# First rows of a routed MoE fetched by token number, and another order of expert passes

## The chip, the cores and the metric

One core of one Trainium2 chip (trn2). The metric is the device time of one execution in microseconds (us); lower is better. The engines are TensorE (PE), VectorE (DVE), ScalarE (ACT), GpSimd (POOL) and SyncE (SP); SP only issues DMAs and waits. ACT and POOL issue DMAs too.

## The reference

A two-layer encoder in float32 over 528 positions (16 meta tokens and 512 frames) of width 1024:

```python
h = x + retention(rms_norm(x), w_in, w_out)      # layer 0
h = h + hier_moe(rms_norm(h), ...)
k, v = shared_kv(h)                              # then layer 1
h = h + swa_sink_attention(rms_norm(h), ..., k, v)
h = h + hier_moe(rms_norm(h), ...)
out = rms_norm(h)

# hier_moe: 4 groups of 4 experts; top-1 group, top-2 experts inside it
expert_idx = g_sel * 4 + top_2(softmax(e_logits[g_sel]))
weights    = g_w * top_p / sum(top_p)
y[token]   = sum over its 2 experts e of weight * (silu(t @ w_gate[e]) * (t @ w_up[e])) @ w_down[e]
```

An expert has 2 MB of gate and up weights and 1 MB of down weights; 16 experts in each of two layers are 100 MB.

## The kernel before

**Retention (to about 500 us)** runs on PE without a gap worth naming. Its last products, `W1_01`, `W1_23` and `W1_4` (token tiles 0 and 1, tiles 2 and 3, the meta tile), come in this order; DVE adds each to `h`, ACT squares (`squares`), POOL makes the deviation (`deviations`), DVE normalizes (`norm_tile`) into `xn`.

**Routing** (`experts` on every engine, once a layer, 5 token tiles in layer 0 and 4 in layer 1). PE transposes each tile (`transposed`), DVE scales it (`feature_major`), PE makes the logits. DVE takes the maxima in a chain of some 30 small steps, each waiting for the one before, up to the masks (`mask_ready`, L1752). PE counts the tokens of each expert before each token (bank 2, `RK`, L1040 and L1042). From the counts DVE works out the slot of each token's two choices: experts get blocks of 64 rows ("pairs") and of 32 rows ("singles"). It writes `slot_i` (L1846), builds `one_hot` (L1851, L1854), then the tables `e_of` of experts by block (L1877).

**Rows by slot.** POOL scatters each token's row of `xn` twice into DRAM `slot_rows` by `slot_i` (L2179, 10 indirect DMAs in layer 0, 8 in layer 1). Pass 0 doesn't wait for that: PE multiplies `one_hot` by `xn` (L1057, 10 or 8 float32 products of 512 columns, two records each in the trace), which leaves the first 128 slots' rows in PSUM banks 0 and 1 (`X0`), and ACT copies them to `xg`. The rows of all other passes are read from `slot_rows` by ACT's queue (`load_rows`) after all scatters.

**Passes** (`ROUNDS` = 12, each 128 rows). PAIRS_IN_PASS = (2, 1, 2, 1, 1, 2, 2, 1, 0, 2, 2, 0): a pass holds n pairs and 4 - 2n singles. PE, for k from 1: `gate_up(k)` (64 records, L1080), `hidden_to_features(k - 1)` (L1087), `rows_to_features(k + 1)` (L1068), `down_project(k - 1)` (L1099). DVE scales the transposed rows (`widen`, L1547).

**Weights** lie in six slots, expert number j in slot j mod 6. Five are filled with a guess (`GUESSED`: all but slot 3) while routing runs. Slot 3 has its 2 MB where `xn` lies, and SP loads it after all scatters. SP loads number j + 6 into the slot of number j when the pass with single j is through: gate and up after that pass's `gate_up`, down after its `down_project`. In SP's program the loads stand in the order of the passes. Before the guessed weights are used, a conditional DMA loads another expert where the guess was wrong; POOL issues such conditional DMAs for the singles (`singles_weights`), and a pass with singles waits for those of the pass in which the same numbers were pairs (`weights_arrived`). SP also loads the first half of the attention's `w_q` after pass 9 of layer 0.

**After the passes** POOL gathers both choices' rows of each token from `slot_out` (L2211) and DVE adds them.

Of the kernel before, what the change touches and what calls it, by code (L numbers as in the profile page):

```python
# [19 lines left out]
D = 1024  # L20
KT = D // 128
# [16 lines left out]
ROWS_SLOT = 3  # L38
GUESSED = [4, 5, 0, 1, 2]
# [6 lines left out]
PAIRS_IN_PASS = (2, 1, 2, 1, 1, 2, 2, 1, 0, 2, 2, 0)  # L46
# [48 lines left out]

def most_blocks(tokens):

    return max((2 * tokens + (BLK - 1) * m) // BLK for m in range(2, EXPERTS + 1))
# [3 lines left out]
assert PASSES[0] == [("pair", 0), ("pair", 1)] and PASSES[-1] == [("single", EXPERTS - 4 + n) for n in range(4)]  # L102
# [10 lines left out]
NCONST = C_DECAY + HEADS * N_META  # L113
# [6 lines left out]
def tables():  # L120
# [15 lines left out]
    c[:, C_EPS] = EPS  # L136
    r = np.zeros((128, NRT), f)
# [103 lines left out]
def build(nc, a, out):  # L241
# [4 lines left out]
    with ctx:  # L246
# [23 lines left out]
        slot_g = sb("slot_g", [128, 2, 5], I)  # L270
        ps = ctx.enter_context(nc.psum_tensor("ps", [128, 8, 512], F))
# [89 lines left out]
        logit_f = arena[:, cv.at:cv.at + POS]  # L361
# [11 lines left out]
        one_hot = xg[:, 1, 0:640].rearrange("p (t s) -> p t s", t=5)  # L373
        xgT = x_words[:, 2 * D:4 * D].rearrange("p (n k c) -> p n k c", n=2, k=KT)
        cv.at = 5 * D + KT * POS
        gat_at = {0: 14336, 1: 16384, 2: 27392, 3: 10240}
        gat = [(x_words[:, 0:2 * D] if t == META else arena[:, gat_at[t]:gat_at[t] + 2 * D]).rearrange("p (n c) -> p n c", n=2)
# [27 lines left out]
        slot_out = nc.dram_tensor("slot_out", (LATE, D), F).ap()  # L405

# [16 lines left out]
        MOE_TILES = [[0, 1, 2, 3, META], [0, 1, 2, 3]]  # L423
# [21 lines left out]
        def moe_plan(l):  # L445
            fl.phase([(f"m{l}_{t}", 2 * (n % 2)) for n, t in enumerate(MOE_TILES[l])])
            fl.phase([(f"LT{l}_{t}", 4 + n % 2) for n, t in enumerate(MOE_TILES[l])])
            fl.phase([(f"LG{l}", 6), (f"RK{l}", 2), (f"X0_{l}", 0)])
# [44 lines left out]
        def sigs(names, tag):  # L493
# [5 lines left out]
        mo = [sigs("eg_in eg_out d_in d_out mask_ready eb_ready slot_ready scattered "  # L499
                   "tanh_done y_out0 y_out1 x_in0 x_in1 "  # L500
                   "gathered0 gathered1 gathered2 gathered3 gathered4 gath_used gather_ready late_ready", f"_{l}") for l in range(2)]
        gu_in, down_in = ([sem(f"{n}{s}") for s in range(W_SLOTS)] for n in ("gate_up_in", "down_in"))
# [12 lines left out]
        def gu(k):  # L515

            return {0: ring[:, 0], 1: gu_arena[:, 0], 2: gu_arena[:, 1], 3: gu_rows, 4: ring[:, 1], 5: ring[:, 2]}[k % W_SLOTS]
# [55 lines left out]
        def out_chunk_used(eng, n):  # L573

            if n % 2:
                fl.wait_full(eng, f"W{n // 2}_4")
            else:
                eng.wait_ge(wo_used, n // 2 + 1)
# [19 lines left out]
        G44 = POSN  # L598
# [7 lines left out]
        B_ROWS, B_HID, B_YA, B_YB = 0, 5, 6, 7  # L606

# [15 lines left out]
        def rows_loaded(k):  # L623

            return groups_until(k, 1)
# [64 lines left out]
        def _(sp):  # L690
# [41 lines left out]
            def first_weights(l, ready):  # L732
# [4 lines left out]
                rest = [j for j in (0, 1, 2, 4, 5) if j not in ready]  # L737
# [6 lines left out]
                for j in (2, 4, 5):  # L744
                    down_weights(l, j, j)

            def experts(l, beside=lambda k: None):
# [5 lines left out]
                for j in sorted(GUESSED):  # L753
# [7 lines left out]
                fl.wait_full(sp, f"X0_{l}")  # L761
# [23 lines left out]
            first_weights(0, {4: chunk_used(2), 5: lambda: None, 0: chunk_used(3)})  # L785

            def attention_loads(k):
# [3 lines left out]
                if k == last_use(5) + 1:  # L791
                    sp.dma_start(ring[:, W_Q[0]], a["w_q"][0]).then_inc(q_in[0], 16)
# [14 lines left out]
            first_weights(1, {5: lambda: fl.wait_full(sp, f"Qa{NT - 1}"), 0: lambda: fl.wait_full(sp, f"Qb{NT - 1}"),  # L807
# [12 lines left out]
        def _(pe):  # L820
# [158 lines left out]
            for hf in range(2):  # L979
                groups = [(f"W{hf}_01", (0, 1)), (f"W{hf}_23", (2, 3)), (f"W{hf}_4", (META,))]  # L980
                for c in range(2):
                    n = 2 * hf + c
                    pe.wait_ge(y_split, HEADS if hf or c else HEADS - 1)
# [26 lines left out]
            def experts(l):  # L1010
# [25 lines left out]

                n = EXPERTS * (5 - l)
# [21 lines left out]
                last.then_inc(full[0], 1)  # L1059
# [3 lines left out]
                def rows_to_features(k):  # L1063
                    if k:
                        pe.wait_ge(m[f"x_in{k % 2}"], rows_loaded(k))
# [46 lines left out]
                rows_to_features(1)  # L1112
                for k in range(1, ROUNDS):
# [161 lines left out]
        def _(act):  # L1275
# [114 lines left out]
            def experts(l, ready):  # L1390
                m = mo[l]
                squares(MOE_TILES[l], nrm[f"_m{l}"], moe_junk[l], ready)
                for t in MOE_TILES[l]:
# [4 lines left out]
                act.wait_ge(m["eg_in"], 1)  # L1398
                nc.scalar.activation(view(EG, 5 - l, 4), view(EG, 5 - l, 4), ACT.Exp).then_inc(m["eg_out"], 1)
                act.wait_ge(m["d_in"], 1)  # L1400
                nc.scalar.activation(view(DX, 5 - l), view(DX, 5 - l), ACT.Exp).then_inc(m["d_out"], 1)
# [42 lines left out]
                fl.wait_full(act, f"X0_{l}")  # L1444
                nc.scalar.activation(xg[:, 0, :], flat(ps[:, 0:2, :]), ACT.Copy).then_inc(free[0], 1)
                act.wait_ge(m["scattered"], 16 * 2 * (5 - l))
                load_rows(1)
# [843 lines left out]
```

## Time and profile before

| | |
|---|---|
| median of 3 runs | 1155.47 us (1153.18 to 1155.6) |
| the profiled execution, its own time | 1156.74 us |
| its span | 1155.1 us |
| PE busy | 1061.4 us, 92% of the span |
| moved by DMA | 200.87 MB |
| DMA queues q1 (SP, POOL's direct ones), q10 (ACT), q0 (POOL's indirect ones) | 151.26, 31.63, 17.04 MB |

A busy PE is not PE at its peak: the records overlap. Times in the traces are microseconds from the start of the span. "Idle before" of a record names what ended the engine's wait. The chain of waits is followed back from the last instruction.

### The profile page before, as it was taken

The numbers are of one execution on the slowest core, as the hardware profiler recorded it, in microseconds if no ns is written. First come the engines' busy times: TensorE is split into PE (matmuls) and PEld (weight loads), VectorE is DVE, ScalarE is ACT, GpSimd is POOL, SyncE is SP. The second block draws the span as 40 slices with busy tenths as digits, with TensorE's granted clock in tenths as the row PEclk, the third lists the DMA queues.
The fourth block names the chain that finished last, engine by engine and source line by source line (L and its number), as shares of the span: only waits on it lengthen the run. The fifth ranks groups of instructions, "written<-read, shape, count | busy, mean of one in ns | idle before, by whom it ended". The sixth has DMA issues, their size and how long they took to land.

```text
span 1155.1 us, 16343 instructions
## 1 busy us (share of the span) xinstructions
PE 1061.4 (92%) x6528; PEld 669.8 (58%) x6528; DVE 465.7 (40%) x831; ACT 248.4 (22%) x479; POOL 238.7 (21%) x232
## 2 busy tenths in 40 slices
PE   4999999999999999987899997989998987999992
PEld 3989979979988877763333332445444453333331
DVE  6400424234236651046223225657547736132217
ACT  5122133114214321020011111314214410011111
POOL 5323314305314524003000005510000002000005
PEclk8999999999999999998899998999999998999996
DMA  7232223114114121366799896130003057899946
GB/s 296 74 128 74 74 80 121 54 45 155 56 37 164 37 73 73 146 264 278 249 358 395 339 397 232 73 146 1 1 1 146 1 233 312 319 366 354 374 198 230
DMA packets 34836, 200.87 MB, mean 174 GB/s; under 512 B 4352, under 2 KB 4480, under 8 KB 25808
## 3 DMA queue, kind: packets, MB, share of 16 engines
q1 hardware_dynamic: 21168, 151.26, 33.9%
q10 hardware_dynamic: 8864, 31.63, 7.7%
q0 software_dynamic: 4736, 17.04, 4.0%
q8 instruction: 47, 0.77, 0.3%
q14 instruction: 21, 0.17, 0.0%
HBM read 303.59 MB, written 28.44 MB: 287 GB/s over the span
## 4 chain that ended last, share of the span: by engine, by line
PE 78%; DVE 13%; ACT 3%; issue 3%; DMA 2%; POOL 1%; POOLq 0%; ACTq 0%; DVEq 0%
PE ps L843 29%; PE ps L1080 15%; PE ps L1099 7%; PE ps L968 4%; PE ps L1204 4%; PE ps L1146 3%; PE ps L849 2%; DVE arena L2075 2%; PE ps L1068 2%; DVE arena L2072 2%; PE ps L1057 2%; PE ps L1018 1%; PE ps L912 1%; ACT arena L1507 1%; PE ps L1164 1%
## 5 line engine op out<-in xcount | busy, mean ns | idle before, releaser
L843 PE MATMUL ps<-x_hi,ring_r 128*128 128x264 f32 x1024 | 190.9, 287 | 2.5 <-DVE xT L1547 2.5
L2155 POOL TENSOR_TENSOR ring_r<-ring,ring_r 128x1024 fp32r<-128x1024 f32 x56 | 134.8, 2422 | 272.3 <-ACT ring_r L1296 272.3
L843 PEld LDWEIGHTS ps<-x_hi,ring_r 128*128 128x128 f32 x1024 | 160.2, 189 | 3.1 <-issue 2.9
L1080 PE MATMUL ps<-arena,xT 128*32 128x512 f32 x864 | 157.8, 600 | 0.0
L1080 PE MATMUL ps<-ring,xT 128*32 128x512 f32 x672 | 143.7, 602 | 5.9 <-DVE xT L1547 5.9
L843 PE MATMUL ps<-xT_r,ring_r 128*128 128x264 f32 x512 | 146.1, 285 | 0.0
L1547 DVE TENSOR_TENSOR xT<-ps,gains 128x512 f32<-128x512 f32 (+1 forms) x76 | 47.1, 661 | 188.4 <-PE ps L1068 178.5
L843 PE MATMUL ps<-ring_r,x_hi 128*128 128x512 f32 x320 | 100.7, 396 | 0.0
L843 PEld LDWEIGHTS ps<-xT_r,ring_r 128*128 128x128 f32 x512 | 96.9, 189 | 0.1
L1099 PE MATMUL ps<-arena 128*32 128x512 f32 x624 | 87.3, 595 | 4.3 <-ACT arena L1421 4.3
L1296 ACT ACTIVATE ring_r<-ring 128x1024 fp32r<-128x1024 f32 x56 | 57.9, 1054 | 118.1 <-PE ps L843 70.8
L1080 PEld LDWEIGHTS ps<-arena,xT 128*32 128x32 f32 x864 | 41.6, 111 | 54.9 <-issue 54.4
L1080 PEld LDWEIGHTS ps<-ring,xT 128*32 128x32 f32 x672 | 37.9, 111 | 60.7 <-issue 60.2
L843 PEld LDWEIGHTS ps<-ring_r,x_hi 128*128 128x128 f32 x320 | 60.1, 188 | 13.8
L2143 POOL TENSOR_SCALAR var<-ss 128x1 f32<-128x1 f32 (+1 forms) x23 | 8.8, 384 | 237.9 <-ACT arena L1284 230.3
L1164 PE MATMUL ps<-ring,xT 128*128 128x512 f32 x128 | 56.1, 595 | 0.0
L968 PE MATMUL ps<-arena 128*128 128x264 f32 (+4 forms) x256 | 47.8, 334 | 0.0
L1099 PEld LDWEIGHTS ps<-arena 128*32 128x32 f32 x624 | 22.6, 109 | 43.1 <-issue 41.4
L1284 ACT ACTIVATE arena<-h 128x1024 f32<-128x1024 f32 (+1 forms) x23 | 24.3, 1057 | 103.3 <-DVE h L1936 48.0
L1421 ACT ACTIVATE arena<-ps 128x256 f32<-128x256 f32 x24 | 9.2, 384 | 167.5 <-PE ps L1087 162.9
L968 PEld LDWEIGHTS ps<-arena 128*128 128x128 f32 (+1 forms) x256 | 41.1, 189 | 6.8
L1507 ACT ACTIVATE arena<-arena 128x256 f32<-128x256 f32 x64 | 31.6, 494 | 62.6 <-DVE arena L2080 62.6
(266 smaller groups left out, 1567.9 us busy)
## 6 DMA issues: line engine op xcount, KB each, us to landing
arena<-in_w_gu SPq DMA_DIRECT2D x22, 2048.0 KB, 14.7
ring<-in_w_gu SPq DMA_DIRECT2D x20, 2048.0 KB
arena<-in_w_down SPq DMA_DIRECT2D x36, 1024.0 KB
arena<-in_w_gu POOLq DMA_DIRECT2D x18, 2048.0 KB
ring<-in_w_gu POOLq DMA_DIRECT2D x14, 2048.0 KB
arena<-in_w_down POOLq DMA_DIRECT2D x26, 1024.0 KB
ring<-in_w_ret SPq DMA_DIRECT2D x48, 512.0 KB, 3.6
ring<-in_w_ret_out SPq DMA_DIRECT2D x16, 512.0 KB, 4.4
```

Of the source, the lines that this page charges most:

```text
L843: last = mm(dst, a_parts[x], b_parts[y], start=(start and n == 0), stop=(stop and n == 2))
L968: last = mm(ps[:, b + g, c - lo:HALF], v_tm[0:r, t, 128 * m:128 * m + 128], scores_of(t)[0:r, c - 128 * t:hi - 128 * t], start=(t == 0), s ...
L1080: last = mm(ps[cols, b, :], xgT[:, k % 2, c, cols], by_row(gu(j))[:, c, :], start=(c == 0), stop=(c == KT - 1))
L1099: last = mm(ps[cols, b, :], hidT[:, c, cols], down(j)[:, c, 512 * n:512 * n + 512], start=(c == 0), stop=(c == 1))
L1146: last = mm(ps[0:rows(t), b, :], xTk[:, k, col0(t):col0(t) + rows(t)], w_kv[:, k, :], start=(k == 0), stop=(k == KT - 1))
L1164: last = mm(ps[:, b, :], xT[:, k, col0(t):col0(t) + 128], w_q[c][:, k, :], start=(k == 0), stop=(k == KT - 1))
L1204: last = mm(ps[:, b + c, :], oT1[:, k, :], w[:, k, :], start=(k == 0), stop=(k == KT - 1))
L1284: nc.scalar.activation(junk[0:r], h[0:r, t, :], ACT.Square, accum_out=ss[0:r, t:t + 1]).then_inc(sig["sq_done"], 1)
L1296: nc.scalar.activation(w_hi[to][:, m], w_raw[slot][:, m], ACT.Copy).then_inc(hi_made, 1)
L1507: nc.scalar.activation(P[:, hd, :], P[:, hd, :], ACT.Exp, bias=nmx[:, hd:hd + 1], accum_out=sm[:, hd:hd + 1]).then_inc(p_exp, 1)
L1547: return V_.tensor_tensor(dst[:, 4 * g:4 * g + 4, c0:c0 + r], src, gains[:, gain, 4 * g:4 * g + 4].unsqueeze(2).to_broadcast([128, 4, r]), ...
L2155: G.tensor_tensor(w_lo[slot][:, m], w_raw[slot][:, m], w_hi[to][:, m], ALU.subtract).then_inc(lo_made, 1)
```

## The change

Pass 0 gets no rows from PE any more. The normalized rows are also stored as they are, by token, in DRAM `token_rows` (ACT's queue, 5 and 4 stores of up to 512 KB). For passes 0, 1 and 2, `one_hot[k]` (slots of pass k) is multiplied by one column of token numbers; ACT casts the 128 sums to `token_i`, and POOL gathers 128 rows by them from `token_rows` into `xg`. DVE works out the slots that lie in pairs first (`first_place`), builds `one_hot[0]`, then the two rows of `e_of` that SP needs, then `one_hot[1]`, and only then the other slots, `slot_i` and `one_hot[2]`.

The order of passes starts 2, 2, 0, 2, 1 pairs, so that each of the first three passes is one run of slots. Slot 5 instead of slot 3 has its weights in the place of `xn`. In layer 0 the meta tile comes third: `W1_4` ahead of `W1_23`. ACT instead of DVE scales the features of pass 0. PE multiplies constants in four places.

```diff
-PAIRS_IN_PASS = (2, 1, 2, 1, 1, 2, 2, 1, 0, 2, 2, 0)
+PAIRS_IN_PASS = (2, 2, 0, 2, 1, 2, 2, 1, 0, 2, 2, 0)
-ROWS_SLOT = 3
-GUESSED = [4, 5, 0, 1, 2]
+ROWS_SLOT = 5
+GUESSED = [0, 1, 2, 3, 4]
+GATHERED = 3
-        MOE_TILES = [[0, 1, 2, 3, META], [0, 1, 2, 3]]
+        MOE_TILES = [[0, 1, META, 2, 3], [0, 1, 2, 3]]
 # SP: the rest of slot 5, and w_q
                 sp.wait_ge(mo[l]["scattered"], 16 * 2 * (5 - l))
-                fl.wait_full(sp, f"X0_{l}")
                 gate_up_weights(l, ROWS_SLOT, e, cond=wanted)
-                if k == last_use(5) + 1:
+                if k == last_use(3):
                     sp.dma_start(ring[:, W_Q[0]], a["w_q"][0]).then_inc(q_in[0], 16)
 # PE
+                constant_products(5)
                 pe.wait_ge(m["mask_ready"], 1)
...
-                for _ in range(9):
-                    mm(ps[:, 4, :], ident, con[:, 0:512], start=True, stop=True)
-                pe.wait_ge(m["slot_ready"], 2)
-                for c in range(2):
-                    for i, t in enumerate(tiles):
-                        last = mm(ps[:, c, :], one_hot[0:rows(t), t, :], xn[0:rows(t), t, 512 * c:512 * c + 512],
+                def tokens_of(k):
+                    pe.wait_ge(hot_ready, GATHERED * l + k + 1)
+                    for i, t in enumerate(tiles):
+                        last = mm(ps[:, B_TOKENS[k], 0:1], one_hot[k][0:rows(t), t, :], con[0:rows(t), C_TOKEN + t:C_TOKEN + t + 1],
                                   start=(i == 0), stop=(i == len(tiles) - 1))
+                    last.then_inc(tokens_made, 1)
+                constant_products(5)
+                tokens_of(0)
+                constant_products(3)
+                tokens_of(1)
+                constant_products(1)
...
                 rows_to_features(0)
                 gate_up(0)
                 rows_to_features(1)
+                tokens_of(2)
 # ACT
+                def store_rows(n):
+                    t = MOE_TILES[l][n]
+                    act.wait_ge(nrm[f"_m{l}"]["xn_done"], n + 1)
+                    act.dma_start(token_rows[128 * t:128 * t + rows(t), :], xn[0:rows(t), t, :]).then_inc(rows_stored, 16)
...
+                def first_features():
+                    round_full(act, l, B_ROWS, 0)
+                    for c in range(KT):
+                        last = nc.scalar.activation(xgT[:, 0, c, :], ps[:, c // 4, 128 * (c % 4):128 * (c % 4) + 128], ACT.Copy,
+                                                    scale=gains[:, G_MOE[l], c:c + 1])
+                tokens_of(0)
+                tokens_of(1)
+                first_features()
                 tanh_of(0)
-                load_rows(2)
+                tokens_of(2)
                 for k in range(1, ROUNDS):
-                    load_rows(k + 2)
+                    if k > 1:
+                        load_rows(k + 2)
                     hidden_of(k - 1)
                     tanh_of(k)
                     results_of(k - 1)
+                    if k == 1:
+                        act.wait_ge(m["scattered"], 16 * 2 * (5 - l))
+                        load_rows(k + 2)
 # DVE, in routing, after D_, ID and P1
+                step(V_.scalar_tensor_tensor(v(PC, nt, 16), per_expert(P0), float(PAIR), pos, ALU.mult, ALU.add))
+                step(V_.tensor_scalar(v(G64, 16), v(D_, 16), float(PAIR), None, ALU.mult))
+                step(V_.tensor_tensor(v(DBL, nt, 16), pos, per_expert(v(G64, 16)), ALU.is_ge))
+                step(V_.scalar_tensor_tensor(v(PC, nt, 16), v(DBL, nt, 16), float(ENC_D), v(PC, nt, 16), ALU.mult, ALU.add))
... (two products with the choices' masks, two sums over experts: first_place)
+                slots_of_pass(0, first_place)
... (rows 0 and 2 of e_of)
+                slots_of_pass(1, shifted)
... (the rest of the slots as before, slot_i)
+                slots_of_pass(2, shifted)
 # POOL
+                def gather_rows(k):
+                    pool.wait_ge(tokens_read, GATHERED * l + k + 1)
+                    if k == 0:
+                        pool.wait_ge(rows_stored, 16 * (5 * l + len(tiles)))
+                    if k == 2:
+                        round_full(pool, l, B_ROWS, 0)
+                    G.indirect_dma_start(xg[:, k % 2, :], None, token_rows,
+                                         bass.IndirectOffsetOnAxis(token_i[:, l, k:k + 1], 0)).then_inc(rows_gathered[k], 16)
+                gather_rows(0)
+                gather_rows(1)
                 pool.wait_ge(m["slot_ready"], 1)
-                for t in tiles:
+                for n, t in enumerate(tiles):
+                    if n == 2:
+                        gather_rows(2)
```

## Rows read from the trace of the kernel before

**Rows 1.** The page: each engine's busy time and share.

```profile
PE 1061.4 (92%) x6528; PEld 669.8 (58%) x6528; DVE 465.7 (40%) x831; ACT 248.4 (22%) x479; POOL 238.7 (21%) x232
```

**Rows 2.** Timeline, end of retention, layer 0: start, us, engine, line, count [idle before].

```profile
496.61 1.23 DVE L1687 TENSOR_TENSOR h<-ps,h 128x1024 f32<-128x1024 f32 x1 [5.46 <-PE ps L843]
...
504.93 3.18 PE L1018 MATMUL ps<-xT,wr 128*20 128x128 f32 x16 [2.92 <-DVE xT L1547]
```

**Rows 3.** Timeline, routing of layer 0, same columns.

```profile
522.99 0.74 PE L1040 MATMUL ps<-arena,con 128*128 128x96 f32 x2 [5.48 <-DVE arena L1752]
...
523.53 2.21 PE L1042 MATMUL ps<-arena,con 128*128 128x80 f32 x10
...
525.84 0.44 DVE L1775 TENSOR_TENSOR arena<-ps,con 128x272 f32<-128x272 f32 x1 [1.77 <-PE ps L1042]
...
535.38 0.17 DVE L1846 CAST slot_i<-arena 128x10 int32<-128x10 f32 x1
...
536.56 1.40 DVE L1854 SCALAR_TENSOR_TENSOR xT<-con,arena,xT 128x128 f32<-128x128 f32 x5
...
538.02 9.43 PE L1057 MATMUL ps<-arena,xT 128*128 128x512 f32 x20 [2.63 <-DVE xT L1854]
...
547.33 0.84 POOL L2179 DMA_INDIRECT slot_rows<-arena,slot_i  x1 [0.30 <-issue]
```

**Rows 4.** Chain of waits, passes of layer 0: start, us, what.

```profile
551.13 9.77 PE ps L1080 x64
...
563.39 7.07 PE ps L1080 x64
570.47 0.37 PE ps L1087 x2
570.84 0.87 PE ps L1068 x8
571.71 3.57 PE ps L1099 x32
...
623.05 7.00 PE ps L1080 x64
```

**Rows 5.** Chain of waits, layer 1, routing and passes.

```profile
957.09 0.45 DVE arena L1775
...
968.69 8.85 PE ps L1057 x16
...
981.20 7.07 PE ps L1080 x64
...
1050.42 7.00 PE ps L1080 x64
```

**Rows 6.** POOL's indirect scatters (L2179), from issue to landing.

```profile
DMA to landing us min/median/max: 3.3/4.3/4.8
```

**Rows 7.** POOL's indirect gathers (L2211), from issue to landing.

```profile
DMA to landing us min/median/max: 2.8/6.1/6.6
```

**Rows 8.** Groups of ACT by form: count | busy us, mean ns | idle before.

```profile
L1474 ACT ACTIVATE xT<-ps,gains 128x128 f32<-128x128 f32 x32 | 8.7, 381 | 7.6 <-DVE arena L1547 7.6
```

**Rows 9.** Timeline of SP's DMA issues, passes of layer 0.

```profile
570.78 0.33 SPq L679 DMA_DIRECT2D ring<-in_w_gu  x1
...
606.22 0.94 SPq L679 DMA_DIRECT2D ring<-in_w_gu  x2
...
672.41 0.46 SPq L792 DMA_DIRECT2D ring<-in_w_q  x1
```

**Rows 10.** All DMA queues from 600 to 620 us, passes of layer 0.

```profile
DMA packets 889, 8.45 MB, mean 423 GB/s; under 512 B 108, under 2 KB 108, under 8 KB 455
```

**Rows 11.** Chain of waits, after the last pass of layer 0.

```profile
694.67 6.03 DMA slot_out<-arena
```

**Rows 12.** Windows: length, busy PE, PEld, DVE, ACT, POOL, granted clock, DMA share, GB/s.

```profile
529.00:536.00 7.00, 6.39 (x15) 2.56 (x13) 6.42 (x37) 0.00 (x0) 0.14 (x1) 0.98 0.02 7
...
550.00:555.00 5.00, 3.87 (x20) 1.15 (x24) 0.98 (x2) 0.00 (x0) 0.00 (x0) 0.50 0.46 107
```

More of the change, by code:

```diff
@@ L93, in groups_until, with first_slot @@
     return 16 * sum(len(row_groups(p)) for p in range(first, k + 1) if p % 2 == k % 2)
+def first_slot(k):
+    (_, slots), = row_groups(k)
+    return slots.start
 def most_blocks(tokens):
@@ L101 @@
 assert most_blocks(POS) <= 3 * EXPERTS and ROUNDS % 2 == 0
-assert PASSES[0] == [("pair", 0), ("pair", 1)] and PASSES[-1] == [("single", EXPERTS - 4 + n) for n in range(4)]
+assert PASSES[:2] == [[("pair", 2 * k + n) for n in range(2)] for k in range(2)]
+assert PASSES[2] == [("single", n) for n in range(4)] and PASSES[-1] == [("single", EXPERTS - 4 + n) for n in range(4)]
 assert all(pass_of("pair", j) < pass_of("single", j) for j in range(EXPERTS))
@@ L575, in out_chunk_used @@
             if n % 2:
-                fl.wait_full(eng, f"W{n // 2}_4")
+                fl.wait_full(eng, "W0_4" if n == 1 else "W1_23")
             else:
@@ L736, in first_weights @@
                     gate_up_weights(l, j, j)
-                rest = [j for j in (0, 1, 2, 4, 5) if j not in ready]
+                rest = [j for j in GUESSED if j not in ready]
                 for j in rest[:2]:
@@ L1035, in experts, with constant_products @@
                 last.then_inc(full[6], 1)
+                def constant_products(n):
+                    for _ in range(n):
+                        mm(ps[:, B_YB, :], ident, con[:, 0:512], start=True, stop=True)
+                constant_products(5)
                 n = EXPERTS * (5 - l)
@@ L1695, in _ @@
                 V_.tensor_tensor(hh, ps[SHORT:SHORT + N_META, b, :], hh, ALU.add).then_inc(free[b], 1)
+            add_rows(0, "W0_01", 0)
+            add_rows(0, "W0_23", 2)
+            add_meta(0)
+            add_rows(1, "W1_01", 0)
+            for n in range(2):
+                norm_tile(nrm["_m0"], n, MOE_TILES[0][n], xn)
+            add_meta(1)
+            norm_tile(nrm["_m0"], 2, META, xn)
+            add_rows(1, "W1_23", 2)
             def experts(l):
@@ new lines, in experts, with slots_of_pass @@
+                step.wait()
+                for n in range(2):
+                    step.done(V_.tensor_reduce(first_place[:, n, 0:nt], in_pairs[:, n], X, ALU.add))
+                step.wait()
+                iota = con[:, C_IOTA:C_IOTA + 128]
+                def slots_of_pass(k, where):
+                    for t in range(nt):
+                        step.done(V_.tensor_scalar(one_hot[k][:, t, :], iota, where[:, 0, t:t + 1], None, ALU.is_equal))
+                    step.wait()
+                    for t in range(nt):
+                        last = V_.scalar_tensor_tensor(one_hot[k][:, t, :], iota, where[:, 1, t:t + 1], one_hot[k][:, t, :],
+                                                       ALU.is_equal, ALU.add)
+                    last.then_inc(hot_ready, 1)
@@ L2175, in experts @@
                     pool.wait_ge(s_zeroed, 32 * HEADS)
-                for t in tiles:
+                for n, t in enumerate(tiles):
+                    if n == 2:
+                        gather_rows(2)
                     r = rows(t)
```

154 lines of the change are left out of this document (83 added, 71 removed).

## Prediction

> **What bounds the kernel now.** I read the page first. PE is busy for 92% of the span [rows 1], so the question is where PE waits, and whether the change shortens that or adds to it. The chain of waits says where: inside retention and inside the passes it is PE alone; around routing it hops between DVE, PE and ACT. In layer 0 PE waits 5.48 us for the masks and 1.77 us of DVE time pass until the counts are in; from then DVE works 12.1 us (525.84 to 537.96) until `one_hot` is ready, PE multiplies for 9.4 us, and pass 0 starts at 551.13 [rows 3, 4]. In layer 1 the same stretch runs from 957.09 to 981.20 [rows 5]. Third, the timeline ahead of that: PE waits 2.92 us for DVE before the first logits, because DVE normalizes two more tiles and adds the meta tile first [rows 2]. Fourth, a pass: 7.07 + 0.37 + 0.87 + 3.57, near 11.9 us, all PE [rows 4]. Last the DMA side, which PE's 92% hides: in a stretch of the passes all 16 engines together move 423 GB/s, filled [rows 10], while ahead of the scatters they stand idle (share 0.02) [rows 12]. Weights are 50 MB a layer, so passes are PE's by a small margin only.
>
> **Part 1, tile order.** `W1_23` ends last, near 500.3 instead of 496.6, its add of 1.23 us ends at 501.6, and DVE scales tile 0 at once (1.3). Logits start near 502.9 instead of 504.93, and without 2.92 us of idle time the first tile's logits may run in 1.9 instead of 3.18 us. The five row stores lie beside this on ACT's queue, the last landing 20 us before anyone needs them. Between -1.5 (norms of the last two tiles now come between the scalings) and -3.3 I take -2.7. Layer 1 keeps its order: 0.
>
> **Part 2, constant products ahead of the masks.** Ten records in the 5.48 us in which PE waits. They keep PE at 2.4 GHz, so that counting (0.74 + 2.21 us, after idling) takes some 1.7. I take -1.2 and -0.9; if the clock were at 1.2 GHz there, they would end 3 us after the masks. Bounds -1.4 and +3.
>
> **Part 3, the first slots ahead of all others.** After the counts: the comparison (0.44), a sum, scan and minimum, seven steps of 0.2 to 0.4 us, and ten `one_hot` steps (2.4 us, as now: 535.5 to 537.96), about 5.8 us where there were 12.1: -6.3. In layer 1 11.6 becomes 5.2: -6.4.
>
> **Part 4, one column instead of 512.** Removed: from 538.02 to 551.13, 13.1 us (12.5 in layer 1). Added: ten records of one column, priced by the counting products, 0.22 each: 2.0 (1.6 in layer 1; below, 1.3); ACT's cast 0.25; start of POOL 0.3; the gather; transposes 1.1; eight ACT steps; 0.15. The gather is 512 KB by indirect DMA. Full scatters land in 4.3 us, gathers at the end of a layer in 6.1, but those queue behind each other [rows 6, 7]. I take 5. ACT's eight steps start every 0.27 us with 0.38 for the last: 2.2 [rows 8]. Sum 11.0 and 10.7: -2.1 and -1.9. The gather of pass 1 follows 4.6 us of DVE later and its products end 0.1 before the first rows land, so this cover is just used up.
> The Trainium skill, *DMA: Bandwidth & Descriptors*, section "Anatomy of one DMA", gives 2.0 us and the bytes at 436 GB/s, an estimate of 3.2 us for this gather where the rows have 4.3 and 6.1. By it the rows would land 1.8 us sooner and PE would still be in the second token product: nothing would be gained.
>
> **Where pass 0 starts.** Layer 0: 2.7 + 1.2 + 6.3 + 2.1 = 12.3 earlier, at 538.8. Layer 1: 9.2 earlier, at 972.0. That is the whole gain, 21.5 us. Now what it triggers.
>
> **Part 5, into pass 2.** The third token product (2.0 us) comes after the transposes of pass 1, where PE now idles 1.45 us for DVE: +0.5 and +0.15. PE would reach `gate_up(2)` at 561.1 and 994.0. `slot_i` comes later by the work put ahead of it: near 540.0 and 973.5. POOL issues an indirect DMA every 1.27 us (535.86 to 547.33, nine steps) [rows 3]: four scatters, then it waits for the third tokens (549.6; 982.3), then that gather and six (four) more scatters. The last scatters land near 561.5 and 991.6. Behind them on POOL stand the conditional DMAs: singles 0 to 3 are now in pass 2 and wait for those of pass 1, which wait for those of pass 0. Bounds for such an empty DMA are 0 and, from the shortest direct landing, some 2 us; with 2 I get 563.5 in layer 0, so +2.4, and 0 in layer 1. The gather of pass 2 lands near 554 and 988, before its turn. ACT stands in its queue at the scatters before it loads pass 3's rows; with slot 5's 3 MB in flight they land some 2 to 3 us late, but PE has a longer wait ahead, which takes this up.
>
> **Part 6, the weights' queue.** This is where I expect the gain to go. Now numbers 6 and 7 are loaded from 570.78, the end of pass 1's `gate_up`, 8 and 9 two passes later, 10 from 606.22 [rows 9], and the down weights of 8 and 9 come behind number 10. With four singles in pass 2, SP issues gate and up of 6, 7, 8, 9 after `gate_up(2)`, their down weights after `down_project(2)`, and number 10, needed in pass 6, behind all eight. That is 4 x 2.1 + 4 x 1.05 + 2.1 = 14.7 MB, and rows in and out of 3.5 passes at 1.05 MB, 3.6: 18.3 MB. At 423 GB/s 43.3 us [rows 10]; with issue and flow 2.5 and the receipt, 46. PE needs only 40.9 from the end of `gate_up(2)` to pass 6. So from 570.4 the weights are there at 616.4, and slot 5, loaded only after the scatters and ahead in the queue, makes it 617.5 (in layer 1 1047.5). Before, pass 6 starts at 623.05 and 1050.42 [rows 4, 5]. Of 12.3 and 9.2 there remain 5.5 and 2.9: -8.4.
> The rule that speaks against the change is in the same page of the Trainium skill, "Issuing engines are not separate DMA queues": a gather on POOL's queue or a store on ACT's adds no bandwidth. The rows agree so far as all queues together stay at 423. With its ceiling of 436 GB/s the sum would be 1.3 us less in each layer, an estimate.
>
> **Part 7, clock.** In layer 0 pass 0 takes 9.77 us where all others take 7.07, since the clock granted was 0.50 (1.2 GHz) after short waits; layer 1 had the same waits and no drop [rows 4, 5, 12]. A drop costs 2.7. There are now four such places, pass 0 and pass 6 of either layer; my count above has none, the run before has one (which is in its 623.05). I take 1.4 drops: +3.8, bounds 0 and 10.8.
>
> **Part 8, `w_q`.** From 672.41 it moves behind pass 11, just ahead of the last store of results, on the path now with 6.03 us [rows 9, 11]. 2.1 MB beside a 0.5 MB store and POOL's gathers: 0 if they take turns without loss, 4 if the gathers are shifted by most of its 5 us. I take +1.5.
>
> **Sum.** -8.4 + 3.8 + 1.5 = -3.1 on the profiled execution's own 1156.74: 1153.6. The median of the runs is 1.3 lower, so 1152.4.
>
> **The rivals.**
> *The passes keep pace.* If number 10 is there in time (a full queue does better than 423, or less has to move), pass 6 starts at 611.3 and 1041.8 and -20.3 stays; with half the clock cost and `w_q`, about -16: 1139.5. Against it: it takes 18.3 MB in 38 us, 480 GB/s, and no row shows that.
> *PE's clock eats the rest.* If both waits before pass 0 and both before pass 6 end at 1.2 GHz, +10.8 in place of 3.8, so +3.9: 1159.4. For it: the waits before pass 6 are 5 to 6 us, and after the 5.48 us wait for the masks the clock was low. It decides from three drops on.
> *The first rows come late.* The gather takes 8 us beside the tail of the guessed weights and the stores, or SP's conditional loads for slot 1 hold pass 0. Then pass 0, and all behind it, is 3 us later in each layer: +2.9: 1158.4. Against it: DMA stands idle from 529 [rows 12].
> *The late `w_q` costs its full 4:* 1155.
>
> **How the numbers follow.** Forecast 0.50, its own range 1147 to 1157; passes keep pace 0.17; clock 0.16; late rows 0.10; `w_q` 0.07. A measurement here tells about 0.2% (2.3 us) from nothing. Of the forecast 0.29 lies below that, 0.11 within, 0.10 above; with the first rival 0.46 is faster; same is 0.11 + 0.05 + 0.04 = 0.20; the rest, 0.34, is slower. For 8 in 10 the range reaches into the first rival and over the second and third: 1143 to 1162.
>
> **What would show it.** Right: pass 0 near 539 and 972; on PE a wait before pass 6 released by the load of gate and up weights, some 5 us; a DMA share of 0.9 and more from pass 2 to 6; the first logits near 503. Wrong if PE has no wait at pass 6 (then faster), if pass 2 waits over 3 us for POOL's conditional loads, if token products come out at far more than 2 us, or if pass 0 waits for weights and not for ACT.

## The result and the profile after

The changed kernel takes 1171.8 us (median of 4 runs, 1171.11 to 1172.68) against 1155.49 of the kernel before beside it: ratio 1.0139, 95% interval 1.0127 to 1.0151. It is 16 us slower. The prediction said 1152.4, 1143 to 1162.

The chain of waits of layer 0 after the change (start, length, what; all in us). It begins with the last product of retention and ends in pass 0; the first and last line are cut by the view's ends. Its first L1038 is the second tile's; the logits of the first tile start at 504.30:

```profile
496.00 5.79 PE ps L861 x25
...
501.81 1.23 DVE h L1744
...
507.22 1.92 PE ps L1038 x16
...
521.41 0.46 PE ps L1065 x2
521.88 1.06 PE ps L1067 x10
...
523.03 0.45 DVE arena L1843
...
527.48 1.41 DVE xT L1878 x5
...
528.93 1.46 PE ps L1079 x10
530.42 0.18 ACT token_i L1490
530.60 0.29 issue
530.89 5.51 DMA xT<-token_rows,token_i
...
536.54 1.08 PE ps L1099 x8
537.64 2.18 ACT xT L1495 x8
539.82 0.14 issue
539.96 5.30 PE ps L1111 x21
```

Up to here the change did what it was to do: pass 0 starts at 539.96 where it started at 551.13 [rows 4], 11.2 us earlier. The same chain through the first passes:

```profile
552.47 7.07 PE ps L1111 x64
...
560.79 3.61 PE ps L1130 x32
...
565.66 11.36 DMA xT<-slot_rows
577.01 0.04 issue
577.06 1.97 PE ps L1099 x8
579.03 4.10 PE ps L1130 x32
583.12 6.87 PE ps L1111 x64
...
607.14 7.00 PE ps L1111 x64
...
619.12 8.36 issue
627.48 8.93 PE ps L1111 x64
```

Two waits are new. PE is done with pass 2's `gate_up` and waits 5.46 us for the rows of pass 3; it then waits 8.36 us before pass 6 (L1111 at 627.48, where the kernel before had 623.05 [rows 4]). In layer 1 pass 0 starts at 980.73 (before 981.20, but this layer's routing began 7.6 us late), the wait before pass 3 is 8.61 us, and the one before pass 6 only 0.6; pass 6 starts near 1063.5 instead of 1050.42 [rows 5]:

```profile
970.52 5.78 DMA xT<-token_rows,token_i
976.44 1.96 PE ps L1099 x8
978.41 2.18 ACT xT L1495 x8
980.73 9.79 PE ps L1111 x64
...
1006.47 14.24 DMA xT<-slot_rows
1020.76 1.97 PE ps L1099 x8
1022.73 4.11 PE ps L1130 x32
```

A balance by the starts of passes: routing of layer 0 gives 11.2, its passes 0 to 11 lose 17.6 (pass 11 starts at 688.7, before 682.3), the rest of layer 0 loses 1.2, routing of layer 1 gives 8.0, its passes lose 14.5. That is 14.1 us lost by pass 11 of layer 1; the spans, 1168.9 and 1155.1, are 13.8 apart.

What the DMA engines do between the end of `gate_up(2)` and pass 6 (this view gives busy time of each engine, the granted clock, the DMA share, and GB/s):

```profile
572.00:627.50 55.50, 42.08 (x364) 14.94 (x366) 14.10 (x32) 5.39 (x15) 0.44 (x10) 0.91 1.01 387
```

All 16 engines are busy throughout and move 387 GB/s, not the 423 of [rows 10]: 21.5 MB, of which 16.9 on the weights' queue and 4.5 on ACT's. The sum of the prediction had 18.3 MB at 423. While the rows of pass 3 are on their way, from 566 to 577, the queues moved:

```profile
q1 hardware_dynamic: 272, 3.14, 73.0%
q10 hardware_dynamic: 313, 1.15, 28.3%
```

The columns are packets, MB and share. SP (q1) had issued slot 5's 3 MB at 565.29 and 565.91, ACT (q10) a store of results at 565.21 and the rows at 565.66. Both queues got about as many packets (from 568 to 576, 217 each), but q10's hold 3.7 KB on average and q1's 11.5. So ACT's queue, with 0.5 MB of store ahead of 0.5 MB of rows, moved 0.1 MB a microsecond. The Trainium skill, *DMA: Bandwidth & Descriptors*, section "Queues, rings and completion order", says that each DMA engine goes round the queues packet by packet; 313 packets beside 272 agree with it.

### The profile page after: what moved, and what is told of

Its sections match the earlier page's. It is cut to its first block, busy times and chain, and to the rows that moved or that the text cites. A ratio compares the mean times of both kernels' runs of the same rounds, so it can differ in the third digit from the quotient of the medians.

```text
span 1168.9 us, 16499 instructions
## 1 busy us (share of the span) xinstructions
PE 1061.4 (91%) x6566; PEld 672.2 (58%) x6566; DVE 475.5 (41%) x881; ACT 251.5 (22%) x499; POOL 242.6 (21%) x238
## 4 chain that ended last, share of the span: by engine, by line
PE 74%; DVE 12%; DMA 7%; issue 3%; ACT 3%; POOL 0%; ACTq 0%; POOLq 0%; DVEq 0%
PE ps L861 29%; PE ps L1111 13%; PE ps L1130 7%; PE ps L986 4%; DMA xT<-slot_rows 4%; PE ps L1236 4%; PE ps L1178 3%; PE ps L867 3%; PE ps L1099 2%; DVE arena L2163 2%; DVE arena L2160 2%; PE ps L930 1%; ACT arena L1565 1%; DVE h L2024 1%; PE ps L1196 1%
## 5 line engine op out<-in xcount | busy, mean ns | idle before, releaser
L1111 PE MATMUL ps<-ring,xT 128*32 128x512 f32 x768 | 162.7, 620 | 13.7 <-issue 8.9
L1111 PE MATMUL ps<-arena,xT 128*32 128x512 f32 x768 | 160.8, 609 | 1.0 <-DVE xT L1605 1.0
L1605 DVE TENSOR_TENSOR xT<-ps,gains 128x512 f32<-128x512 f32 (+1 forms) x72 | 44.4, 658 | 190.9 <-PE ps L1099 183.3
L1111 PEld LDWEIGHTS ps<-ring,xT 128*32 128x32 f32 x768 | 43.9, 114 | 92.4 <-issue 91.9
L1111 PEld LDWEIGHTS ps<-arena,xT 128*32 128x32 f32 x768 | 42.4, 112 | 36.0 <-issue 35.6
```

What stands on the lines that cost most here:

```text
L1111: last = mm(ps[cols, b, :], xgT[:, k % 2, c, cols], by_row(gu(j))[:, c, :], start=(c == 0), stop=(c == KT - 1))
L1605: return V_.tensor_tensor(dst[:, 4 * g:4 * g + 4, c0:c0 + r], src, gains[:, gain, 4 * g:4 * g + 4].unsqueeze(2).to_broadcast([128, 4, r]), ...
```

## The experiments

All ratios are to the kernel before, run on the same chip beside each group; intervals are at 95%. The changed kernel has 1.0139. The start of a pass is that of its `gate_up`'s first product.

**e1: all scatters ahead of the third gather.**

```diff
                 for n, t in enumerate(tiles):
-                    if n == 2:
-                        gather_rows(2)
...
+                gather_rows(2)
                 pool.wait_ge(m["eb_ready"], 2)
```

> The changed kernel, with one line moved: POOL issues the gather for pass 2 behind all scatters instead of behind the first four. Queue theory (the scatters land at 565.3 where they landed before 552, so slot 5's 3 MB and all loads behind them start late and the DMA engines stay full until pass 6): the scatters land near 557.5, slot 5 is loaded before ACT asks for the rows of pass 3, PE's wait before the transposes of pass 3 falls from 5.5 and 8.8 us to under 1 us and pass 6 starts some 6 us sooner in both layers: about 1160 us. Clock theory (the loss is low clock after waits, wherever they are): waits only move to pass 2, whose rows come 1 to 2 us later; 1170 to 1173 us. Theory that row loads are slow whatever lies beside them: the wait before pass 3 stays over 4 us, 1169 to 1172 us.

1174.3 us, 1.0164 (1.0134 to 1.0194). None of the three was right. The wait before pass 3 is gone in both layers, as the queue theory said, but PE waits 8.4 and 9.0 us before pass 6, which starts at 626.3 and 1064.7: 1.2 us sooner in one layer and 1.2 later in the other. And `gate_up(1)` starts at 556.15 instead of 552.47, at low clock: the third token product, ten products of one column, is strung out over 5.8 us while the scatters run. Nothing that the profile shows released PE in these gaps:

```profile
550.92 0.38 PE L1079 MATMUL ps<-con,arena 128*128 128x1 f32 x2 [1.25 <-issue]
552.34 0.16 PE L1079 MATMUL ps<-con,arena 16*128 16x1 f32 x1 [1.03 <-issue]
553.05 1.08 PE L1079 MATMUL ps<-con,arena 16*128 16x1 f32 x4 [0.56 <-issue]
```

**e2: slot 5's 2 MB of gate and up weights never loaded.**

```diff
+                _, never = expert_of(0)
...
-                gate_up_weights(l, ROWS_SLOT, e, cond=wanted)
+                gate_up_weights(l, ROWS_SLOT, e, cond=never)
```

> The changed kernel, but the 2 MB of gate and up weights of number 5 are never loaded (its products are made from what lies there; all else is loaded and done as before). Queue theory: 2 MB less ahead of the rows of pass 3 and of numbers 6 to 10, some 5 us of DMA at 423 GB/s in each layer: the wait before pass 3 nearly goes and pass 6 starts 5 us sooner, so 1161 to 1163 us. If the waits hang on when PE releases the slots and not on bytes: the first wait goes, and the second grows by as much, 1169 to 1172 us.

1166.12 us, 1.0093 (1.0062 to 1.0124). 5.7 us less, but of an expected 9 to 11. The wait before pass 3 falls to 1.2 and 0.9 us. Pass 6 starts at 620.3 in layer 0, 7 us sooner, yet PE still waits there: 6.5 and 7.7 us. So slot 5's bytes count, they are most of what delays the rows of pass 3, and they are not the whole cause of the wait before pass 6.

**e3: only the order of passes changed, with the old front.**

```diff
-ROWS_SLOT = 3
+ROWS_SLOT = 5
-PAIRS_IN_PASS = (2, 1, 2, 1, 1, 2, 2, 1, 0, 2, 2, 0)
+PAIRS_IN_PASS = (2, 2, 0, 2, 1, 2, 2, 1, 0, 2, 2, 0)
-                if k == last_use(5) + 1:
+                if k == last_use(3):
```

> The kernel before (rows of pass 0 as products of 512 columns, no gathers by token), with only the order of passes 2, 2, 0, 2, 1 and with it slot 5 in place of slot 3 as the one loaded after the scatters, and w_q behind pass 11. Theory that the order costs by itself (four numbers' weights asked for at once after pass 2, 12 us later than the first two before): pass 0 at 551 and 981 as before, pass 6 near 629 and 1056, so +12 us and 1.5 for w_q: 1165 to 1170 us. Theory that the order is harmless and only the early start with late scatters hurts: 1155 to 1158 us.

1180.89 us, 1.022 (1.0189 to 1.025), 24 us slower than the kernel before. The order costs by itself, and more than the range said. Its chain in layer 0 has no wait before pass 3, and this before pass 6 (the last line is cut by the view's end; the whole `gate_up` takes 8.61 us):

```profile
612.07 7.00 PE ps L1081 x64
...
624.15 8.01 issue
632.16 8.16 PE ps L1081 x57
```

Layer 1 has 7.74 us at the same place. Of the 24 us these two and their clock are some 19, and w_q 2 to 3. This is the largest finding: the change is two changes, an order that costs about 24 us from the old front, and an early front that brings pass 0 about 19 us forward in the two layers together. Of these 19 only some 9 are left at the end (1180.89 to 1171.8): the waits take the rest. The front with the old order was not run, since the order is what makes the first three passes one run of slots.

**e4: tile order and constant products in the kernel before; e14: tile order alone.**

```diff
-        MOE_TILES = [[0, 1, 2, 3, META], [0, 1, 2, 3]]
+        MOE_TILES = [[0, 1, META, 2, 3], [0, 1, 2, 3]]
+                for _ in range(5):      # e4 only
+                    mm(ps[:, 7, :], ident, con[:, 0:512], start=True, stop=True)
                 pe.wait_ge(m["mask_ready"], 1)
```

> The kernel before, with only the tile order of layer 0 (meta tile third, W1_4 ahead of W1_23) and five constant products ahead of the masks (parts 1 and 2 of the prediction). By my terms 2.7 us and 1.2 in layer 0, 0.9 in layer 1; scatters and all loads move with it, so the gain is kept: 1150.5 to 1151.5 us. Theory that the passes of the kernel before are already set by the weights' queue whatever starts earlier: at most 1 us, 1154.5 to 1155.5 us.

> The kernel before with the tile order of layer 0 alone (part 1), no constant products. My term: masks, slots and scatters 2.7 to 3.1 us sooner in layer 0, nothing in layer 1, so 1152.5 to 1153 us against 1155.5 to 1156.5. If the weights' queue or the clock takes it up: no change.

e4: 1154.27 us, 0.9983 (0.997 to 0.9996), some 2 us. e14: 1152.97 us, 0.997 (0.9958 to 0.9983), 3.2 us and near its term. The constants did not add to that. PE's timeline in e4 shows the reason (the bracket is the idle time before and what ended it):

```profile
533.79 14.02 PE L1061 MATMUL ps<-arena,xT 128*128 128x512 f32 x20 [4.46 <-DVE xT L1866]
```

and in e14:

```profile
535.75 9.63 PE L1059 MATMUL ps<-arena,xT 128*128 128x512 f32 x20 [2.27 <-DVE xT L1864]
```

With constants `one_hot` is ready 2.0 us sooner, but the constant products behind the counts also end sooner; PE stands idle for 4.46 us, and the products of pass 0's rows run at a granted clock of 0.50 (534 to 542) for 14.0 instead of 9.6 us.

**e5: number 10's gate and up weights ahead of the down weights of 8 and 9.**

```diff
                         gate_up_weights(l, j, e, cond=wanted)
+                        if j == 10:
+                            for late in (8, 9):
+                                e, wanted = chosen[late]
+                                down_weights(l, late, e, cond=wanted)
```

> The changed kernel, but SP issues the down weights of numbers 8 and 9 behind the gate and up weights of number 10, which pass 6 needs first, instead of ahead of them. Queue theory (number 10 is asked for only at the end of gate_up(4) and stands behind 4.2 MB of down weights asked for one pass earlier): 2.1 MB less ahead of it is 5 us at 423 GB/s, so the wait before pass 6 falls from 8.4 to some 3.5 us in layer 0 and as much in layer 1; the wait before pass 3 stays: 1160 to 1163 us. Theory that all queued bytes share the engines, so that order in SP's queue does not matter: 1170 to 1173 us.

1162.07 us, 1.0052 (1.0033 to 1.007), 9.7 us less than the change from one move in SP's queue. SP's DMAs, and PE's chain past pass 6, where no wait stands any more:

```profile
597.93 1.23 SPq L702 DMA_DIRECT2D arena<-in_w_down  x2
605.16 0.33 SPq L698 DMA_DIRECT2D ring<-in_w_gu  x1
605.77 0.94 SPq L702 DMA_DIRECT2D arena<-in_w_down  x2
606.99 0.33 SPq L698 DMA_DIRECT2D arena<-in_w_gu  x1
```

```profile
609.91 7.00 PE ps L1115 x64
...
618.16 3.57 PE ps L1134 x32
621.73 0.16 PE ps L1143
621.89 7.00 PE ps L1115 x64
```

Order in the queue matters. The wait before pass 3 stayed in sum (8.6 and 5.2 us, for 5.5 and 8.6); that it is what gives number 10 its time is argued here, and e13 bears on it.

**e6: the order 2, 2, 0 four times.**

```diff
-PAIRS_IN_PASS = (2, 2, 0, 2, 1, 2, 2, 1, 0, 2, 2, 0)
+PAIRS_IN_PASS = (2, 2, 0, 2, 2, 0, 2, 2, 0, 2, 2, 0)
```

> The changed kernel with the pass order 2, 2, 0 four times over, so that pass 6 needs numbers 8 and 9 and no longer 9 and 10; numbers 10 to 13 are asked for after pass 5 and needed from pass 7. Order theory (the wait before pass 6 comes from number 10 alone): no wait before pass 6, the waits before pass 3 stay at 5.5 and 8.8 us; 10 and 11 land some 5 us ahead of pass 7: 1153 to 1157 us. Theory that the DMA engines are behind by some 8 us whatever the order: the wait moves to pass 7, 1168 to 1173 us.

1154.14 us, 1.0003 (0.9978 to 1.0027): the whole loss is gone by this line. The ten runs lie in two groups, six from 1151.6 to 1155.5 and four from 1160.3 to 1161.9; the trace is of the first, and what parts them is open. The waits before pass 3 stay (5.4 and 3.7 us). Pass 6 starts at 618.1 and 1045.2, pass 7 at 630.1 and 1057.3, 12 us apart, so no wait moved to pass 7.

**e7: the third token product inside `gate_up(0)`.**

```diff
                     for c in range(KT):
+                        if k == 0 and c == 5:
+                            tokens_of(2)
```

> The changed kernel, but PE makes the third token product inside gate_up(0), after five of its eight steps, and ACT casts it before the tanh of pass 0, so that POOL's third gather and the scatters behind it start some 5 to 6 us sooner. Theory that the scatters' lateness (they stand on POOL behind the third gather) makes slot 5's loads and PE's wait before pass 3: scatters land near 559.5, wait before pass 3 under 1 us, pass 6 follows the end of gate_up(2) by 49 us instead of 55: 1157 to 1160 us. Theory that more DMA work beside pass 1 slows PE there (as with all scatters first): pass 1 starts 3 to 5 us later and eats it: 1168 to 1173 us.

1165.12 us, 1.0074 (1.0051 to 1.0096). 6.7 us of an expected 12 to 15. The third gather is issued at 547.26 instead of 552.66, pass 6 starts at 619.5, 48.8 us behind the end of `gate_up(2)`, as said. But the rows of pass 3 still take 9.35 us to land and PE waits 3.4 us: ACT issues them behind the results of pass 0, at 565, however early the scatters are. In layer 1 PE's wait before pass 3 falls from 8.6 to 1.5 us, and the one before pass 6 grows from 0.6 to 7.9.

**e8: e7, the order of e6, and w_q behind the last gathers.**

```diff
-                if k == last_use(3):
-                    sp.dma_start(ring[:, W_Q[0]], a["w_q"][0]).then_inc(q_in[0], 16)
...
             sp.wait_ge(mo[0]["gathered3"], 32)
+            sp.dma_start(ring[:, W_Q[0]], a["w_q"][0]).then_inc(q_in[0], 16)
```

> Three edits together: the third token product inside gate_up(0), the pass order 2, 2, 0 four times over, and the first half of w_q loaded behind the last gathers of layer 0 instead of beside the last store of results. If the three causes are the ones named and independent: no wait before pass 3 (7 us a layer with its clock), none before pass 6 (10 and 9 us), and 3 us less at the end of layer 0: 1135 to 1141 us, ahead of both kernels. If the DMA engines are the bound of passes 3 to 7 in any order, a wait of 5 us or more stands somewhere before pass 7 in each layer: 1148 to 1156 us.

1144.04 us, 0.9897 (0.988 to 0.9913), faster than both kernels. Passes start at 539.9, 552.2, 563.9, 577.6 and then every 12.0 us. It missed its range because pass 0 still runs at low clock in both layers, pass 3 waits 1.8 us, and pass 10 of layer 1 waits 2.0 us.

**e9: SP loads the rows of pass 3 ahead of slot 5's weights.**

```diff
                 sp.wait_ge(mo[l]["scattered"], 16 * 2 * (5 - l))
+                round_full(sp, l, B_ROWS, 1)
+                for place, src in row_groups(3):
+                    sp.dma_start(xg[place, 1, :], slot_rows[src, :]).then_inc(mo[l]["x_in1"], 16)
                 gate_up_weights(l, ROWS_SLOT, e, cond=wanted)
```

> The changed kernel, but SP itself loads the rows of pass 3 as soon as the scatters have landed, ahead of slot 5's 3 MB; ACT no longer does. Theory that these rows are slow because they share the engines with slot 5's load: they land within 4 us of 565.3, PE's wait before pass 3 falls from 5.5 and 8.8 us to 2 us at most (then for slot 5's weights), and passes 3 to 5 start 4 to 6 us sooner. Queue theory for the rest: number 10's weights land no sooner, so the wait before pass 6 grows by what the first lost, and the total moves by 0 to -3 us: 1168 to 1171.5 us. Theory that the two waits add up independently: 1158 to 1161 us.

1176.65 us, 1.0182 (1.0161 to 1.0203). The rows, issued at 562.61, land in 3.3 us instead of 11.4, PE waits for nothing before pass 3, passes 3 to 5 of layer 0 start 7.5 us sooner, and all but 2.3 us of it is waited out before pass 6:

```profile
599.76 7.00 PE ps L1114 x64
...
611.58 0.16 PE ps L1142
611.74 13.46 issue
625.20 9.70 PE ps L1114 x64
```

Layer 1 has 12.82 us there. The length of the wait does not set what the clock costs behind it: `gate_up(6)` takes 9.70 us after 13.46, 8.38 after 12.82, and in e12 9.97 after 4.51, for 8.93 after 8.36 in the changed kernel. The median is 5 us worse than the change's, though the profiled span is only 1.7 us longer (1170.6 against 1168.9); the expectation (0 to -3) had neither.

**e10: e8 with constant products in PE's idle places; e11: e10 with e9's edit; e12: e11 with the change's own order and e5's edit.**

```diff
-                constant_products(5)
+                constant_products(6)
                 tokens_of(0)
...
-                constant_products(1)
+                constant_products(1 + l)
...
                 rows_to_features(0)
+                constant_products(2)
                 gate_up(0)
```

> Third tokens early, periodic order and w_q last (the run before that took 1144.0), and constant products in PE's idle places ahead of pass 0: one more before the first token product, one more before the transposes of pass 0 in layer 1, two while ACT scales the features. Clock theory: pass 0 is granted 2.4 GHz and takes 7.1 us instead of 9.8 and 9.9, nothing behind it takes this back, -5.4 us: 1138 to 1140 us. Theory that the clock was lost earlier, in the wait for the masks or for the gather, and these don't bring it back: 1143 to 1146 us.

> As the run with constants, and SP loads the rows of pass 3 ahead of slot 5's weights. The last wait of the first layer's passes (1.8 us, before pass 3) goes: 1.5 to 2.5 us below the run with constants, 1136 to 1138 us. If slot 5's weights, now later, hold pass 3 instead: no change against it.

> The change's own pass order 2, 2, 0, 2, 1, with the down weights of 8 and 9 behind number 10, third tokens early, constants, w_q last, SP loading the rows of pass 3 first. If the order of passes is not itself at fault, but number 10's place in SP's queue and the late rows: as fast as with the periodic order, 1136 to 1141 us. If the order leaves too little time for number 10: a wait of 3 us or more before pass 6 in each layer, 1143 us or more.

e10: 1143.31 us, 0.9888 (0.9872 to 0.9905); e11: 1145.24 us, 0.9892 (0.9868 to 0.9916); e12: 1148.93 us, 0.993 (0.9911 to 0.9949). In e10 the clock came back, as PE's timeline shows (a pair of products in 0.62 us, not 1.07):

```profile
537.47 1.88 PE L1058 MATMUL ps<-con 128*128 128x512 f32 x4
540.00 0.62 PE L1112 MATMUL ps<-ring,xT 128*32 128x512 f32 x2 [0.64 <-ACT xT L1496]
```

Pass 1 then starts 11.1 and 10.7 us behind pass 0 instead of 12.3 and 12.4. Yet the medians of e8 and e10 differ by only 0.7 us, and the intervals of their ratios overlap. In layer 0 nothing is left of it at pass 3 (578.0, in e8 577.6): `gate_up(1)` in layer 0 takes 8.9 us instead of 7.1, at full clock and with scatters beside it, and pass 3 in layer 1 waits 2.45 us for its rows. e11 took pass 3's wait away and was not faster. e12 shows the order's own share when all else is mended: pass 6 waits 4.5 and 4.4 us, and it is 5.6 us behind e10.

**e13: e5 and e9 together.** Both diffs above.

> The changed kernel with two edits together: the down weights of 8 and 9 behind number 10's gate and up weights, and SP loading the rows of pass 3 ahead of slot 5's. The first alone took 1162.1, the second alone was no gain. Queue theory: without the 5.5 and 8.8 us of waiting before pass 3, PE reaches pass 6 at some 616 and number 10's weights, now 2.1 MB nearer, land near 619 to 620: 2 to 4 us better than the first edit alone in each layer, 1154 to 1158 us. If the waits only trade places in every form: 1160 to 1164 us. If they are independent: 12 us and more, under 1151 us.

1164.27 us, 1.0068 (1.0044 to 1.0093), so no better than e5 (1.0052). The waits only trade places: in layer 0 `gate_up(3)` waits 3.6 us for slot 5's weights, pass 6 waits 6.1 us, and starts at 620.7 where e5 had 621.9; in layer 1 pass 6 waits 7.5 us.

**e15: w_q behind the last gathers, alone.** Diff as in e8.

> The changed kernel with the first half of w_q loaded behind the last gathers of layer 0 instead of beside the last store of results (part 8). The store lands 6.2 us after its issue instead of 8.9, the gathers follow, nothing waits for w_q: 2.5 to 3.5 us, 1168.5 to 1169.5 us. If the layer's end is set by the gathers' own time: 1171 to 1173 us.

1168.04 us, 1.0103 (1.0084 to 1.0123): 3.8 us less by the medians. The last store, in e15 and in the changed kernel:

```profile
698.48 5.92 DMA slot_out<-arena
```

```profile
701.12 8.87 DMA slot_out<-arena
```

## Why the prediction was wrong

**The front (parts 1 to 4): right in sum, pass 0 at 539.96 for 538.8, and in layer 1 8.0 us gained for 9.2.** Part 1: the first logits start at 504.30, for 502.9, and the first tile's take 1.92 us, for 1.9. The 1.4 us between lie ahead of the part: in this trace retention's last product ends near 501.8, for 500.3. The count starts 1.6 us earlier than before, for 2.7. PE comes to the transposes behind retention 1.5 us later here than before, 0.9 in e14 and 0.1 in e4, and there the counts start 2.2 and 3.0 us earlier: from the end of retention on, the tile order gives 3.1 us in all three. Why retention ends at different times is not shown. Part 2: counting takes 1.5 for 2.8 us, 1.3 gained for 1.2; that PE's idle time can cost its clock where long products follow is seen in e4. Part 3: from the counts to `one_hot` 5.9 us, for 5.8. Part 4: 11.03 us from `one_hot` to pass 0, for 11.0, with token products of 1.46 (for 2.0) and a gather of 5.51 and 5.78 (for 5). In layer 1 it is 11.75, for 10.7: the transposes ran at low clock (1.96 us, for 1.1). The cover named for it was not quite there: with the row stores beside them the guessed weights keep the DMA engines busy until some 534.5, not 529. The gathers took 0.5 and 0.8 us more than the term, so the rival of late first rows (3 us a layer) is not what happened; that the weights caused these 0.5 and 0.8 is argued.

**Part 5 is the first step that failed, by its size**, in the sentence that the rows of pass 3 "land some 2 to 3 us late, but PE has a longer wait ahead, which takes this up". The scatters land at 565.3 for 561.5, as the third gather ahead of them is issued at 552.66 for 549.6 (pass 0 at low clock). The rows then share the engines with 3 MB in larger packets and take 11.4 and 14.2 us, for about 7; PE waits 5.5 and 8.6 us, and the transposes and the down products behind the wait run at low clock. e9 shows it: issued ahead of slot 5's load and of ACT's store of results they land in 3.3 us. e2 parts the two: with the store still ahead and 2 of slot 5's 3 MB gone, 1.2 and 0.9 us of wait are left. That the wait ahead takes this up was right in kind: e9 takes the wait before pass 3 away and the kernel is no faster. What the lateness cost is in the next part, since slot 5's load stands ahead of number 10. The term for POOL's conditional loads (+2.4) did not occur.

**Part 6 named the mechanism and sized it too small.** It said that number 10 stands behind eight other loads and that pass 6 waits; it waits. But pass 6 starts at 627.5, for 617.5, and in layer 1 at 1063.5, which is 1055.9 without the 7.6 us by which that layer began late, for 1047.5. So the two come 10.0 and 8.4 us later than forecast, of which the front has 1.2 and 1.1; the profiled execution's own time was 17.5 us above the 1153.6 forecast for it. In layer 0 the 10.0 are 0.8 by which `gate_up(2)` ends late (571.2 for 570.4), 3.0 for the queue without slot 5 (49 us as in e1, e3 and e7 below, for 46), and 6.2 for slot 5's load (7.3 for 1.1). In layer 1 PE lost the time at pass 3 and hardly waits at pass 6; with the first wait gone or small (e1, e7, e9) it stands before pass 6 there too, 9.0, 7.9 and 12.8 us.

Two sizes were off. The rate: 387 GB/s and not 423 over the stretch, which makes 47.3 us of 18.3 MB instead of 43.3. And the bytes: 21.5 MB, since part of slot 5's 3 MB was still queued at 572 and ACT's queue moved 4.5 MB, for 3.6. (That 21.5 / 387 gives the 55.5 us of the stretch proves nothing, as the rate was had by dividing the two.) What shows it is the runs in which slot 5's load is asked for 11 us or more before the end of `gate_up(2)` (e1, e3, e7): 19.0 to 19.5 MB then move at 388 to 400 GB/s, and pass 6 follows by 49.2, 48.9 and 48.8 us, against the 46 of the prediction and the 40.9 that PE needs. In e12, with 2.1 MB of down weights behind number 10, it is 45.3.

The rate came from too short a stretch. The 20 us of [rows 10] had stores and rows in them as well, 1.4 of 8.5 MB (17%, and 21% in the changed kernel), so 423 was not the rate of weights alone. But from 571 to 623 us the kernel before had (same columns as above):

```profile
571.00:623.00 52.00, 52.00 (x469) 18.01 (x468) 15.51 (x34) 6.71 (x17) 0.53 (x12) 1.00 0.95 374
```

That is 374 GB/s at a DMA share of 0.95, an estimate of some 394 for a full one. The DMA engines of the kernel before were busy for 95% of this stretch, so there was little room for more to be asked for at once.

The two failures are not a sum but one budget. e1, e9 and e13 take the first wait away and get it back at pass 6; e5 takes the second away while the first remains. What comes nearest to ending both is to ask for less before pass 6 (e6) and to start the scatters sooner (e7): e8 does both, and of the waits before passes 3 and 6 only 1.8 us in layer 0 is left. With the change's own order and everything else mended, 4.5 and 4.4 us before pass 6 remain (e12). e3 against the kernel before shows that the order costs some 24 us from the old front, e6 against the change that another order with the same front gives back 1.4%, some 16 us.

**Part 7:** lost clock, counted by what passes took above 7.07 and 3.57: 2.7 in pass 0 of layer 1 (in layer 0 the kernel before had it too), 0.5 in the down products and 1.1 in the transposes behind the late rows of pass 3 in both layers, 1.9 in pass 6 of layer 0, together some 8 us, for 3.8 and within its bounds. Three of its four places came at low clock (pass 0 of both layers, pass 6 of layer 0). The rival "PE's clock eats the rest" is thus true in its mechanism, but by 4 us and not by 16. **Part 8:** w_q costs 2.8 us by the profiled spans and 3.8 by the medians (e15), for 1.5: the rival with 4 was nearer. **"The passes keep pace"** was the furthest from what happened.

Open: why `gate_up(1)` of layer 0 is 1.8 to 2.2 us longer in e2 and in e9 to e12 (in e2, e9 and e12 with gaps of 0.8 us that nothing in the profile ends), and why e9 is 5 us worse than the change and not equal to it (its longer `gate_up(6)` is 0.8 of that in layer 0).

## What to carry to other kernels

Where transfers are busy 95% of the time behind a busy PE, an order of work is a schedule of bytes: for each release of a buffer write down what is asked for, behind what, by when it is due, at the rate measured over a stretch as long as the one that is planned. Put what is due first in front in its queue, before making anything start earlier. In this kernel a wait taken away ahead of such a bound came back as the next one; take the bound away first and then the waits in front of it.

A change made of two parts, here a front that gains and an order that it asks for, should be run as two. The best version found keeps the new front, and with the order 2, 2, 0 repeated, the third tokens early, w_q last and constants in idle places takes 1143.31 us, 1.1% less than the kernel before; without the constants it is 1144.04, which the intervals don't tell apart.

## What the hardware showed that I had not expected

With all DMA engines busy the throughput was between 334 and 439 GB/s in stretches of 8 us (387 over 55.5 us). What sets it from one stretch to the next is not shown.

Two queues with work got nearly equal numbers of packets (313 and 272), so the one whose packets hold 3.7 KB on average, against 11.5, got 27% of the bytes.

With ten scatters of POOL in flight PE stood still between products that wait for nothing, up to 1.25 us at a time (e1), and `gate_up(1)` stretched by 1.8 us (e10). The profile calls the gaps "issue". The profile lists two instruction queues among the DMA queues (47 and 22 packets in the changed kernel), so late instruction fetches come to mind. But PE's gaps in e1 lie between 548 and 555, and in that trace no packet of these queues moves from 542 to 566; the cause is open.

Constant products that end early can cost the clock: in e4 PE was busy until 529.3, idle for 4.46 us, and then got 1.2 GHz (0.50) for the first 8 us of the products that counted; in e14, 2.27 us idle, the same products took 9.6 us instead of 14.0.
